# Second block of a two-block decoder: linear attention by two heads at once, sums of squares of four heads side by side, the query scale in the exponential, queries ahead of the last gates

## The reference

```python
for l in range(DEPTH):                       # 2 layers
    h = rmsnorm(x, norm_g[l])
    z = h @ w_in[l]                          # 1024 -> 20 column blocks of 128
    (g_q, g_k, g_v, g_lr, g_gate, c_q, c_kv, k_pe, m_gate) = split(z)
    log_a = log_sigmoid(g_lr @ w_gla_gate_up[l] + b_gla_gate[l]) / 16
    o_gla = gla_mix(g_q, g_k, g_v, log_a, gla_norm_g[l]) * silu(g_gate)
    q  = rmsnorm(c_q,  mla_q_norm_g[l])  @ w_uq[l]      # 4 heads x (128 + 64)
    kv = rmsnorm(c_kv, mla_kv_norm_g[l]) @ w_ukv[l]     # 4 heads x (128 + 128)
    q, k = rmsnorm(q, q_head_g[l]), rmsnorm(k, k_head_g[l])   # over the 192 of a head
    q, k = rope on the last 64 of q and k
    o_mla = block_causal_attention(q, k, v) * silu(m_gate)
    x = x + concat([o_gla, o_mla]) @ w_out[l]

# gla_mix: 4 heads, keys 64 wide, values 128 wide, 8 chunks of 64 tokens, b = cumsum(log_a) in a chunk
a_intra = where(causal, (q exp(b)) (k exp(-b))^T, 0)            # scores of a chunk
state   = exp(b_last) * state + (k exp(b_last - b))^T v          # update of a chunk
o       = rmsnorm(a_intra v + (q exp(b)) state_before, norm_g)   # per head
```

## Time and profile before

| | before |
|---|---|
| median of 3 runs | 1964.65 us (1960.3 to 1965.61) |
| the profiled execution's own time | 1965.29 us |
| its span | 1963.5 us |
| mean granted TensorE clock | 0.974 |
| PE busy | 1882.7 us (96%) |
| DVE busy | 1050.5 us (54%) |
| ACT busy | 808.0 us (41%) |
| POOL busy | 36.2 us (2%) |
| DMA, mean | 78 GB/s |

### The profile page before, as it was taken

How to read it: one execution, slowest core, us unless ns; L and a number is a source line. 1 busy time by engine, 2 the same in 40 slices (tenths; PEclk the granted TensorE clock), 3 DMA queues, 4 the chain that set the end, 5 groups by cost and what they waited for, 6 DMA issues and landing times.

```text
span 1963.5 us, 23432 instructions
## 1 busy us (share of the span) xinstructions
PE 1882.7 (96%) x9750; PEld 1533.3 (78%) x9750; DVE 1050.5 (54%) x1609; ACT 808.0 (41%) x1260; POOL 36.2 (2%) x27
## 2 busy tenths in 40 slices
PE   8997899999999999999899999999999899999898
PEld 6886888888888877776688888888778676878775
DVE  5776665454433647666645454335564555564553
ACT  5667553333322545554533333323542324341422
POOL 0000100000000000001000000000000000000000
PEclk9998999999999999999999999999999889999889
DMA  5231232323232221112132323332221111222101
GB/s 192 94 97 44 86 97 86 107 87 107 97 96 86 88 85 51 47 44 72 58 106 86 108 86 107 97 97 76 71 75 55 53 33 32 83 79 65 43 11 43
DMA packets 43498, 153.64 MB, mean 78 GB/s; under 512 B 4833, under 2 KB 4993, under 8 KB 43393
## 3 DMA queue, kind: packets, MB, share of 16 engines
q1 hardware_dynamic: 43392, 152.15, 24.0%
HBM read 150.03 MB, written 2.10 MB: 77 GB/s over the span
## 4 chain that ended last, share of the span: by engine, by line
PE 86%; DVE 7%; ACT 5%; issue 2%; DMA 0%; SPq 0%; DVEq 0%; ACTq 0%
PE bank L425 86%; ACT wh L1089 1%; DVE tmp L1671 1%; DVE wl L1680 1%; ACT tmp L1089 1%; ACT X L1089 1%; DVE tmp L1668 1%; ACT XH L1089 1%; DMA wraw<-in_wstream 0%; DVE acc_q L1668 0%; ACT Y L1089 0%; PE bank L1050 0%; DVE XL L1680 0%; DVE X L1668 0%; DVE sqr L1671 0%
## 5 line engine op out<-in xcount | busy, mean ns | idle before, releaser
L425 PE MATMUL bank<-XH,wh 128*128 128x512 f32 (+1 forms) x1720 | 664.1, 386 | 32.8 <-DVE XL L1680 15.0
L425 PE MATMUL bank<-XL,wh 128*128 128x512 f32 (+1 forms) x1720 | 646.8, 376 | 0.0
L425 PE MATMUL bank<-XH,wl 128*128 128x512 f32 (+1 forms) x1720 | 646.4, 376 | 0.0
L1680 DVE TENSOR_TENSOR wl<-wraw,wh 128x1024 fp32r<-128x1024 f32 x278 | 339.4, 1229 | 321.9 <-ACT wh L1089 321.8
L1089 ACT ACTIVATE wh<-wraw 128x1024 fp32r<-128x1024 f32 x278 | 291.5, 1054 | 346.1 <-PE bank L425 338.0
L425 PEld LDWEIGHTS bank<-XH,wh 128*128 128x128 f32 x1720 | 330.1, 192 | 100.4 <-issue 24.6
L425 PEld LDWEIGHTS bank<-XH,wl 128*128 128x128 f32 x1720 | 329.6, 192 | 58.3
L425 PEld LDWEIGHTS bank<-XL,wh 128*128 128x128 f32 x1720 | 330.3, 192 | 56.5 <-issue 2.6
L425 PE MATMUL bank<-HH,wh 128*128 128x512 f32 (+1 forms) x428 | 162.9, 381 | 10.3 <-ACT PP L1089 10.3
L425 PE MATMUL bank<-HL,wh 128*128 128x512 f32 (+1 forms) x428 | 159.2, 372 | 0.0
L425 PE MATMUL bank<-HH,wl 128*128 128x512 f32 (+1 forms) x428 | 159.1, 372 | 0.0
(11 more groups left out here) (263 smaller groups left out, 2130.5 us busy)
## 6 DMA issues: line engine op xcount, KB each, us to landing
wraw<-in_wstream SPq DMA_DIRECT2D x278, 512.0 KB, 3.5
X<-in_xt SPq DMA_DIRECT2D x8, 256.0 KB, 6.6
out<-X SPq DMA_DIRECT2D x8, 256.0 KB, 2.0
pts<-in_pt SPq DMA_DIRECT2D x4, 256.0 KB, 3.9
cst<-in_consts SPq DMA_DIRECT2D x1, 653.0 KB, 9.4
acc_s<-in_pos SPq DMA_DIRECT2D x1, 256.0 KB, 4.3
prm<-in_params SPq DMA_DIRECT2D x1, 164.0 KB, 8.3
wgu<-in_wgu SPq DMA_DIRECT2D x1, 32.0 KB, 2.3
```

The lines of the kernel that those rows point to most:

```text
L425: return pe.e.matmul(o, l, r, start=start, stop=stop, skip_group_check=True)
L1680: return dve.e.tensor_tensor(o, x, h.bitcast(F32), ALU.subtract)
```

## The change

Seven things change, all in the second block and the same in both layers:

1. **Linear attention by pairs of heads.** Both turns stand together. The update of a pair is 14 matmuls with 64 columns of weights each (before 7 with 64 rows by 128 columns, of whose 256 result columns one half of the rows belonged to the other head). Scores and the products with the states take the two heads of a pair alternately, one in the upper and one in the lower 64 rows. DVE makes a state step for both heads with one instruction of 128 partitions, and the mask of a head with one `copy_predicated` over 512 columns instead of four of 128.
2. **Sums of squares side by side.** `head_sums`: 32 columns of ones are the weights, the squares are the moving side, and head h writes the 32 rows from 32h on. `columns` then brings them to token layout with 4 small matmuls. All four heads of the linear attention are summed once; one POOL root of 128x16 takes the place of two of 128x8.
3. **Key norm** stays by columns: `head_sums`, DVE, ACT Ln and Exp, one DVE Newton step, then `pick` and `pick2` spread it over the partitions.
4. **Query norm** is not spread: its inverse root, with the attention's scale, is `scale=` of the exponential of the attention, one value per query token. DVE multiplies the (negated) row maximum by it, one 128x1 instruction more for each of 16 attention steps in a layer.
5. **Order.** `uq` and the keys move ahead of the last two gate columns, and the norms of k and q are the side work of these. The 16 pieces of `halves()` all fill the attention.
6. `cqh`, `cql`, `ckh`, `ckl` have tiles of their own and are made earlier (`cql` by DVE from PSUM ahead of `columns()`, `ckl` ahead of the evacuation of `gk`).
7. `kpa` and `kpb` (copies of the rope keys in other partitions) are filled by 6 DMAs of SP instead of 2 ACT and 4 DVE copies. The constants grow from 1306 to 1620 columns.

```diff
@@ order of the stream
-        o += grouped(f"in{layer}", KD, list(range(12, 20)), 2)
-        o += grouped(f"uq{layer}", 2, [4, 5, 6, 7, 0, 1, 2, 3], 4)
+        o += grouped(f"in{layer}", KD, list(range(12, 18)), 2)
         o += grouped(f"ukv{layer}", 1, list(range(4)), 4)
+        o += grouped(f"uq{layer}", 2, [4, 5, 6, 7, 0, 1, 2, 3], 1)
+        o += grouped(f"in{layer}", KD, [18, 19], 2)
@@ SP
+            if u == w.at[f"in{layer}", 4, 6] // NU:
+                sp.wait_ge(s.lrk, layer + 1)
+                for r in range(2):
+                    sp.e.dma_start(m.kpa[64 * r:64 * r + 64, :], m.lr[0:64, :]).then_inc(s.kp_in, 16)
+                for r0, r1 in ((0, 32), (32, 0), (64, 32), (96, 0)):
+                    sp.e.dma_start(m.kpb[r0:r0 + 32, :], m.lr[r1:r1 + 32, :]).then_inc(s.kp_in, 16)
@@ PE
+        def head_sums(o, xs, start):
+            for h, x in enumerate(xs):
+                ins = mm(o[32 * h:32 * h + 32, :], m.ONE.broadcast_to([128, 32]), x, start, True)
+            return ins
+        def columns(o, x):
+            for j in range(4):
+                ins = mm(o[:, 4 * j:4 * j + 4], x[:, j * 128:(j + 1) * 128], C("ident")[:, 0:128:32], j == 0, True)
+            return ins
+        def gla_updates(i):
...
+            for n in range(7):
+                r, c = slice(64 * (n % 2), 64 * (n % 2) + 64), n // 2 * 128
+                for hh in range(2):
+                    ins = mm(bank[G_UPD[i][n % 2]][64 * hh:64 * hh + 64, c:c + 128],
+                             m.ket[r, n // 2, i * 128 + 64 * hh:i * 128 + 64 * hh + 64],
+                             m.gv[r, n // 2, i * 256 + 128 * hh:i * 256 + 128 * hh + 128], True, True)
...
+            head_sums(bank[4], m.gsq, True).then_inc(s.gsum, 1)
...
+        queries(4, 5, 6, 7)
+        pe.wait_ge(s.ksq, 4 * layer + 4)
...
+        mm(bank[1][:, :], m.ONE[0:64, :].broadcast_to([64, 128]), m.ckv[0:64, :], True, False)
+        head_sums(bank[1], m.ksq, False).then_inc(s.hsum, 1)
+        queries(0, 1, 2, 3)
...
+            for i in range(2):
+                mm(bank[0][64 * i:64 * i + 64, :], C("halves"), m.lab[:, i, :], True, False)
+            head_sums(bank[0], [m.PT[:, h, :] for h in range(4)], False).then_inc(s.hsum, 1)
...
+        gates(3, norms())
+        pe.wait_ge(s.qvc, layer + 1)
+        pe.wait_ge(s.kn, 6 * layer + 6)
+        by_token("ukv" + L, 0, 4, (4, 5, 6, 7), m.ckh, m.ckl, True, True)
@@ DVE
+                stt(m.states[:, i, n + 1, :], m.states[:, i, n, :], m.eb[:, i, 64 * n + 63:64 * n + 64],
+                    bank[G_UPD[i][n % 2]][:, n // 2 * 128:n // 2 * 128 + 128], ALU.mult, ALU.add).then_inc(s.sts, 1)
@@ DVE, attention step
-            dve.e.reduce_max(nm, o[:, 0:n], AX.X, negate=True).then_inc(s.at_m, 1)
+            t = dve.mark(dve.e.reduce_max(nm, o[:, 0:n], AX.X, negate=True))
+            dve.wait_ge(dve.own, t)
+            c = 96 + 4 * qb + j // 4
+            tt(nm, nm, m.vr[:, c:c + 1], ALU.mult).then_inc(s.at_m, 1)
@@ ACT, behind the last gates
+        act.wait_ge(s.qvc, layer + 1)
+        n = act.mark(fn(m.vr[:, 48:64], m.vr[:, 32:48], ACT.Ln))
+        act.wait_ge(act.own, n)
+        fn(m.vr[:, 48:64], m.vr[:, 48:64], ACT.Exp, scale=-0.5).then_inc(s.hy, 1)
+        table(SILU)
         feed_group("ukv" + L, range(1), range(4, 8))
+        silu(3)
...
             fn(XH[:, h, :], m.gates[:, h, :], ACT.Copy).then_inc(s.mt_h, 1)
         for i in range(4):
             act.wait_ge(s.stream, w.done("ukv" + L, 0, 7, i))
+            fn(m.gv[:, i, :], bank[4 + i][:, :], ACT.Copy).then_inc(s.gv, 1)
+        table(LNEXP)
```

More of the change, by code:

```diff
@@ L109 @@
          "mgl": (640, 128), "scan": (768, 512), "invf": (1280, 1), "sgn": (1281, 1), "mhalf": (1282, 16),
-         "one": (1298, 1), "epsr": (1299, 1), "halves": (1300, 2), "first": (1302, 4)}
-NCONST = 1306
+         "one": (1298, 1), "epsr": (1299, 1), "pick": (1300, 128), "pick2": (1428, 128), "halves": (1556, 64)}
+NCONST = 1620
 class Stream:
@@ L946, in gla, with gates @@
+            pe.wait_ge(s.gt, 4 * layer + 4)
+            columns(bank[5], m.acc_s).then_inc(s.cols, 1)
             yield
-            gla_out(2)
             yield
-            gla_out(3)
+            pe.wait_ge(s.ms_r, layer + 1)
+            for h in range(4):
+                spread_row(bank[G_SPREAD[h]], m.vr[:, 16 + h:32:4]).then_inc(s.ms_sp, 1)
             yield
-            yield from gla_norms(1, (2, 3))
-        side = gla()
-        for g in range(4):
+        def gates(g, side):
             b = (0, 2)[g % 2]
@@ L964, in tensor_program @@
                     next(side, None)
+        side = gla()
+        for g in range(3):
+            gates(g, side)
         for _ in side:
             pass
[L968 to L977 removed]
@@ L1514, in scalar_program @@
                 forget(k - 1)
-            elif k == 3:
-                act.wait_ge(s.lrk, layer + 1)
-                for r in range(2):
-                    fn(m.kpa[64 * r:64 * r + 64, :], m.lr[0:64, :], ACT.Copy).then_inc(s.kpa, 1)
         act.wait_ge(s.r0c, layer + 1)
@@ L2191, in vector_program @@
             pass
+        dve.wait_ge(s.ck_h, layer + 1)
+        less(m.ckl, m.ckv[:, :], m.ckh).then_inc(s.ck_l, 1)
         for i in range(2):
@@ L2314, in vector_program @@
-        tt(m.kpa[:, :], m.kpa[:, :], m.kpa[:, :], ALU.mult).then_inc(s.rope_sq, 1)
+        side = gla()
+        for g in range(3):
+            if g == 1:
+                dve.wait_ge(s.kp_in, 96 * (layer + 1))
+                if layer == 0:
+                    dve.wait_ge(s.sin, 2)
+                    n = dve.mark(ts(m.sinT[:, :], m.sinT[:, :], C("sgn"), None, ALU.mult))
+                    dve.wait_ge(dve.own, n)
+                n1 = rope(m.kr[:, :], m.kpa[:, :], m.kpb[:, :], P("kga" + L), P("kgb" + L), tmp[1], tmp[3])
+            gates(g, side)
@@ L2317, in vector_program @@
         feed_group("ukv" + L, range(1), range(4, 8))
+        for h in range(4):
+            dve.wait_ge(s.mt_h, 8 * layer + h + 1)
+            less(XL[:, h, :], m.gates[:, h, :], XH[:, h, :]).then_inc(s.mt, 1)
         def halves():
@@ L2552, in constants @@
     put("mhalf", -0.5)
-    put("halves", np.repeat(np.eye(2), 64, 0))
-    put("first", np.arange(128)[:, None] < 64)
+    put("pick", i % 32 == 0)
+    put("pick2", (i % 32 == 0) & (i // 32 % 2 == j // 64))
+    put("halves", (i // 64 == j // 32)[:, 0:64])
     put("one", 1.0)
```

554 lines of the change are left out of this document (233 added, 321 removed).

## The result

| | before | after |
|---|---|---|
| median | 1965.13 us (1960.3 to 1966.39, 4 runs) | 1882.41 us (1881.41 to 1884.02, 4 runs) |
| ratio after / before | | 0.9584, 95% interval 0.9566 to 0.9602 |
| span of the profiled execution | 1963.5 us | 1879.9 us |
| mean granted clock | 0.974 | 0.989 |

The change makes the kernel 82.7 us faster.

What follows compares the result with a forecast made beforehand. PE was taken as the bound, busy 96% of the span. Savings of 34.0 us in the last layer and 32.0 in the other, 66 together, took 1965.3 to 1899.3, or 1900 us; range 1886 to 1928.

Steps and rivals of the forecast that it cites:

- the pool of the first layer: Turn to last 96 matmuls: 66.9 us of small products, waits and lost clock in the last layer, taken for both layers.
- the attention taken as fixed: Attention without its 4 output pieces: 40.1 us a layer that any version must do, each piece 1.43 us.
- the wait for ACT with its lost clock: Behind the value projection PE waits about 4.0 us a layer for ACT (bounds 0 and 8); lost clock 2.5.
- the first turn: Layer 0's turn of linear attention, waiting for DVE: about 5.5 us instead of 3.5, a loss of 2.0.
- the part of the change that I had put at 0: Six small DMAs, issued during the keys and queries of linear attention, and the constants: 0 us.
- three signs of being wrong: Head sums over 2 us, wait behind the values over 8 us, or a clock under 0.9 in any gates window.
- The terms of PE's small products: Last layer after the change, us: turns 1.1, updates 2.4, scores 2.1, products 8.1, their sums 5.8, k 3.8, q 2.75.
- Narrow tiles in a row: Rival: 32-column groups and 64-row pairs don't run together; +8 to +18 us a layer, 1916 to 1936; chance 0.12.
- The longer wait with the clock: Rival: wait of 8 us behind the values, then 10 us at half clock; +8 a layer, 1915; chance 0.2.
- Clock at half through the attention: Rival: clock stays at half through attention behind the new wait; +40 us a layer against 34 gained, 1977; chance 0.03.
- DVE's chain: Rival: attention falls behind on DVE through the multiply of the maximum; 5 us a layer, 1910; chance 0.06.
- no new wait, full clock: Low end of the worked-out forecast: no wait behind the values, full clock after it, 2 x 6.5 us less, 1887.

Runs made afterwards that it cites:

- Experiment 6: Kernel before, with the 12 pieces of the output product moved from between the norms into the attention: 1979.9 us, ratio to before 1.0083.
- experiment 8: Changed kernel, with the last two silus and their table load on ACT behind the first two evacuations of the values: 1874.4 us.
- experiment 1: Changed kernel, with one head's products before the other's in updates, scores and products with the states, instead of alternating: 1904.17 us, ratio to before 0.9676.
- experiment 2: Changed kernel, with three more 512-column sums in linear attention, all in the last 32 columns of the array: 1889.07 us.
- experiment 4: Changed kernel, without the multiply of the row maximum and without the scale in the exponential: 1883.23 us.
- experiment 3: Changed kernel, with four multiplies of the row maximum in each attention step instead of one: 1897.14 us.
- experiment 5: Changed kernel, with 12 of the 16 output product pieces ahead of the attention and 4 in it: 1893.51 us.
- experiment 10: Changed kernel, with the last silus behind the first two value evacuations on ACT, and the first layer's linear attention turn 12 matmuls later: 1874.25 us.

## Why the prediction was right in its mechanism and wrong in its size

Four steps of the sum failed: the pool of the first layer (4.3 us), the attention taken as fixed (2.5 in each layer), the wait for ACT with its lost clock (2.7 in each layer), and the first turn (2.7). Of the three signs of being wrong two did not come (head sums 1.00 us, the wait 2.19). The third, a clock under 0.9 in a window of the gates, came only for the few us behind the turn of the first layer, where the clock was at half before the change too; from turn to attention it is 0.96 and 1.00. All three looked for a slower kernel, and the kernel was faster.

**The pool of the first layer.** The sum took "66.9 - 32.9 = 34.0 in the last layer, 32.0 in the other". This step failed. The stretch was worked out in the last layer alone and used for both. The first layer's was 196.1 us long, not 189.9. Of these 6.2, 2.6 were the end of its attention at half clock (the last value product's 2.18 us took 4.28, and the waits before it are the same in both layers), and 2.7 the 12 matmuls and the turn at half clock behind the wait of the earlier trace rows. The rest, 0.9, lies in smaller places. The first went with the change. The second stayed: the turns and the 12 matmuls behind them take 3.5 us more than in the last layer. But this layer lost no clock behind the wait for ACT, where the last lost 1.6, so it is 1.9 longer now: 4.3 of the 6.2 were won beyond the sum.

**The turn of the first layer.** "About 5.5 instead of 3.5, a loss of 2.0": it was 2.77 and 0.28. I had put the multiplies of both halves of `gk` ahead of the first turn, but the second turn waits for its own, only 0.28. The first wait is even shorter than before, with `ckl` (0.6 us) ahead of it, because of the part of the change that I had put at 0. Before, two ACT copies for `kpa` stand ahead of ACT's `wh`, and DVE waits for this `wh`; the change has DMAs for them:

```profile
1431.64 1.27 ACT L1089 ACTIVATE kpa<-lr 64x512 f32<-64x512 f32 x2
1434.03 1.23 DVE L1680 TENSOR_TENSOR wl<-wraw,wh 128x1024 fp32r<-128x1024 f32 x1 [2.12 <-ACT wh L1089]
```

```profile
1431.92 1.23 DVE L1686 TENSOR_TENSOR wl<-wraw,wh 128x1024 fp32r<-128x1024 f32 x1 [0.81 <-ACT wh L1096]
```

DVE waits 1.3 less there, `ckl` takes 0.6 of it back, and the wait of PE is 0.7 shorter (2.77 against 3.48). This is read from the two traces; no run has the copies back.

**The attention.** The sum took "the attention without its 4 output pieces: 45.79 less 4 x 1.43 for 6 matmuls = 40.1" as fixed, and put each of 16 pieces on top at 1.43: 63.0. This step failed too. Without the wait for ACT and the lost clock it took 60.5 (64.21 less 2.19 and 1.5), 2.5 less. Experiment 6 shows the same in the kernel before, where a piece costs 1.19 in the attention. The shown waits (3.0 us before, 1.45 at its end after) are 1.6 of the 2.5. Some of the rest is in the price: behind the same small product the next scores start 1.50 us later with a piece (1815.20 to 1816.70 after) and 0.11 without (1910.50 to 1910.61 before), so a piece adds 1.39. The remainder was not taken apart.

**The new wait.** Right in place and cause (experiment 8), 2.19 instead of 4.0. With it the lost clock, 2.5 forecast, was about 1.5 to 1.6 (6 matmuls and the scores behind it) in the last layer and none in the first.

**The terms of PE's small products** were close in the last layer, forecast against start to start: updates 2.4 and 2.0, scores 2.1 and 2.2, products 8.1 and 7.6, sums with root and spread 5.8 and 5.8, k 3.8 and 4.2, q 2.75 and 2.8, turns 1.1 and 0.8, hand-overs 0.4 and 0.75. Their sum, 26.5 and 26.2, is closer than the terms, since some misses cancel. Experiments 1 and 2 confirm what stands behind them: the order of neighbours in different parts of the array is worth 4.9 us a layer in linear attention, and 3.2 more by the clock that the other order lost in the profiled execution; side by side, a set of four sums takes 1.0 us instead of 3.4 (an estimate, 4 x 0.84).

**In sum,** from 66 to 83.6: the last layer 4.8 more (wait and clock 2.7, attention 2.5, less 0.4 for the stretch in front of it), the first within its stretch 9.2 more (the same 4.8, and 6.2 less 1.9 for its length), and 3.5 ahead of it (2.7 by the turn, 0.8 of an earlier start that stands already in the first block, which the change doesn't touch).

**The rivals.** Narrow tiles in a row: refuted by the timeline and by experiments 1 and 2. The longer wait with the clock: a wait, but a short one. Clock at half through the attention: in the changed kernel it fell at most for some matmuls behind a wait. DVE's chain: not with one multiply (experiment 4), but it was the right place to worry, since three more cost 13.5 us in the two attentions (experiment 3).

**The range** was too narrow on the good side. Its lower end was "no new wait, full clock", 13 us under the forecast, of which 5.4 came. It took the rest of the sum as exact, and had no case for a bigger pool, a cheaper attention or a shorter turn, which together were 12 us.

## What to carry to other kernels

Before a gain is counted twice, measure both places: two layers with the same program differed by 6.2 us here, and most of it was lost clock; after the change they differ by 1.9. A filler between small steps is worth more where other engines' chains are long; when a stage gets cheap, ask what its filler can now cover. Small products belong in pairs of neighbours in different rows or columns of the array, not just in narrow shapes: the same 16 products took 2.00 or 3.39 us by their order.

## What the hardware showed that I had not expected

Two executions may differ where nothing was changed: the first turn of the second block comes anywhere from 1447.8 to 1454.8 us (experiments 8 and 5) in kernels that do the same work up to there. A median of 4 runs can thus move by some us for an edit that does nothing, and stretches of the trace tell small edits apart better.

The clock can fall without any wait. In experiment 1 PE was busy all through the state products in the worse order (3.32 us, 64 of the 128 rows at a time, clock 1.00), and the granted clock was 0.50 for about 3 us of the matmuls behind them. In the changed kernel the same products took 1.93 us and the clock stayed at 1.00.

The clock behind a short wait is not the same each time. Behind the wait of 1.47 us at the first value product in the last layer it stayed at 1.00 in experiment 8, and fell in experiment 10, where this value product took 3.37 us to the next start instead of 2.2. The wait of 2.19 was followed by half clock in the last layer of the changed kernel (the 6 matmuls behind it took 2.72 us) and by none in the first (1.50).

Four fp32 products of 512 columns in four groups of 32 columns take 1.00 us with their switch, and three in one group 2.5. Four in one group would be 3.4 (an estimate, 4 x 0.84), so the gain is a factor of 3.4 of the possible four.
